# Chunks of two on-chip activation tensors laid 64 bytes further apart

## The chip, the cores and the metric

The program runs on one core of one Trainium2 chip. The metric is the device time of one launch in microseconds (us). Two runs of the kernel before took 2256.53 and 2257.57 us, median 2257.05 us. Numbers of the profile are of one execution of the same program.

The engines are TensorE (PE in the profile; its loads of the stationary operand are listed apart, as PEld), VectorE (DVE), ScalarE (ACT), GpSimd (POOL, idle here) and SyncE (SP, which only issues DMAs).

## The reference

What is computed is a stack of two blocks of two layers each on one sequence of T = 256 tokens with D = 1024 channels, in float32. Each layer is

```
h = rmsnorm(x, g1);   x = x + 0.5 * (silu(h @ w1) * (h @ w3)) @ w2       # FFN, 1024 -> 2816 -> 1024
h = rmsnorm(x, g_mix); p = h @ w_in                                       # 8 chunks of 128 channels
x = x + merge(mixers of p, gated by sigmoid(p)) @ w_o
h = rmsnorm(x, g2);   x = x + 0.5 * (silu(h @ w1b) * (h @ w3b)) @ w2b     # FFN again
```

In block 1 the mixers are a Fourier mix, a short convolution and a pooling mix; in block 2 they are a sliding-window attention and a gated linear attention. Block 1 ends with one more rmsnorm. Nearly all arithmetic is in the eight FFNs and in the projections of the mixers.

## The kernel before, in words

**Split products.** TensorE works on float32r operands. To keep float32 accuracy every operand is split into a high part and a low part, and each product is made of three matmuls: high by high, high by low, low by high. Weights arrive by DMA in `raw` (3 slots of 8192 bytes per partition); ScalarE copies a slot into the high half of `split_w` (line 1176), VectorE subtracts to make the low half (line 1646), in a ring of 4 slots.

**Activations, turned.** The normalised input of a stage lies in `xt`: for each of 8 chunks of 128 channels it holds 256 high values and behind them 256 low values per partition, that is 512 float32 or 2048 bytes per chunk. ScalarE writes the high part of a chunk (line 1188), VectorE the low part (line 1661), chunk by chunk, with 256 elements each. The product of the first FFN half, silu(gate) * up, lies in `ht_hi` and `ht_lo`: 22 chunks of 256 values or 1024 bytes each; ScalarE writes a chunk of the first (line 1253) and VectorE one of the second (line 1791).

**Two kinds of product.** They differ in which operand sits in the array (stationary) and which streams through it (moving).

- *FFN, first half* (`hidden_chunks`, lines 666 and 667; for the very first units `hidden_high` and `hidden_low`, lines 677 and 685): weights are stationary, `xt` moves. For each chunk c of `xt` and each of 2 column groups one matmul streams the whole chunk, 512 columns, against the high weights, and one streams its high half, 256 columns, against the low weights. So a chunk is used by 4 matmuls in a row, then comes the next chunk.
- *All else* (`blocks`, lines 602 to 604): 128 columns of the activation are stationary, the weights move, 512 columns at a time. For each chunk and each of 2 token halves there are three matmuls (602: high by high, 603: high by low weights, 604: low by high weights). So a chunk is used by 6 matmuls in a row. The activation is `xt` for the input projections of the mixers, `ht_hi`/`ht_lo` for the second half of an FFN, and small tensors (`bz`, `fq`, `pl`, `mt`, `oa`, `ob`) for the output projections of the mixers.

Every matmul has its own load of 128 stationary columns, 512 bytes per partition. In the trace the load for the next matmul starts together with the matmul at work.

**One odd form.** In block 2 two units of input weights (`kv` and `glr`) are 272 columns wide. Their four chunks lie packed in a slot of `split_w`, that is 272 * 4 = 1088 bytes apart. They are the only moving operands of the float32r kind in this kernel, besides one of 4 matmuls (line 1010), whose chunks don't lie at multiples of 512 bytes from the stationary ones.

**Places in memory.** Tensors are laid one behind the other in each partition, in the order in which `build` makes them, and those of stages that never live together share places (`ffn`, `mix1`, `mix2`). Worked out from the sizes in `build`, `split_w`, `xt`, `ht_hi`, `ht_lo` and all stationary tensors of the output projections start at an address that leaves 128 when divided by 512. Two `spacer` tensors ahead of them hold no data.

**What sets the order.** Each engine runs its own hand-written list; semaphores tie them. Nothing in the lists depends on addresses.

Of the kernel before, what the change touches and what calls it, by code (L numbers as in the profile page):

```python
# [21 lines left out]
F32R = mybir.dt.float32r  # L22
# [5 lines left out]
P = 128  # L28
T = 256
MT = T // P  # L30
D = 1024
DC = D // P
FF = 2816
FG = FF // 256
FC = FF // P
EPS = 1e-6
WARM = 11
PAIR = (0, 2, 1)
SPACER = 40
RAW = 3  # L40
HL = 4

# [133 lines left out]
def build(nc, a, known):  # L176

    ctx = ExitStack()
    counts = Counts()

    def semaphore(name):
        return ctx.enter_context(nc.semaphore(name))
# [7 lines left out]
    with ctx:  # L190
        def sb(stack, name, shape, dt=F32):
            return stack.enter_context(nc.sbuf_tensor(name, shape, dt))


        raw = sb(ctx, "raw", [P, RAW, 2048])
        split_w = sb(ctx, "split_w", [P, HL, 2, 2048], F32R)
        whi, wlo = split_w[:, :, 0, :], split_w[:, :, 1, :]
        x = sb(ctx, "x", [P, MT, D])
        xt = sb(ctx, "xt", [P, DC, 2, T], F32R)
        xt_hi, xt_lo = xt[:, :, 0, :], xt[:, :, 1, :]  # L200
        ident = sb(ctx, "ident", [P, P])

# [10 lines left out]

        sb(ctx, "spacer", [P, SPACER])
        tables2 = ExitStack()
# [16 lines left out]
        first.close()  # L232

        ffn = ExitStack()
        ht_hi = sb(ffn, "ht_hi", [P, FC, T], F32R)
        ht_lo = sb(ffn, "ht_lo", [P, FC, T], F32R)
        gate = sb(ffn, "gate", [P, 2, T])
        up = sb(ffn, "up", [P, 2, T])
        low = sb(ffn, "low", [P, 2, 2, T])
# [92 lines left out]

        raw_in = [semaphore(f"raw_in{r}") for r in range(RAW)]
        hi_done = semaphore("hi_done")
# [37 lines left out]
        def units(e, u, extra=0):  # L372

            return e.unit(u) + 1 + extra

        def loaded(e, u):

            return 32 * (e.unit(u) // RAW + 1) - 16

# [32 lines left out]
        def _(eng):  # L412
# [5 lines left out]
            def load(u, halves):  # L418

                r = e.unit(u) % RAW  # L420
                eng.wait_ge(w_ready, units(e, u))
# [157 lines left out]
        def _(eng):  # L579
# [7 lines left out]
            def blocks(u, block, p, split, chunks, start, stop, used, cols=512, beside=False, ready=True):  # L587
# [5 lines left out]
                if block == 0 and ready:  # L593
                    eng.wait_ge(w_ready, units(e, u, RAW))
                for i, c in enumerate(chunks):
# [13 lines left out]
            def last_blocks(u, p, split, chunks):  # L609

                hi, lo = split
                slot = u % HL
                eng.wait_ge(w_ready, units(e, u, RAW))
                for m in range(MT):
# [1804 lines left out]
```

## Time and profile before

| what | value |
|---|---|
| runs | 2256.53 and 2257.57 us |
| span of the profiled execution, first to last instruction | 2255.2 us |
| that span against the median of the runs, 2257.05 us | 1.85 us less |
| TensorE busy | 2249.8 us |
| VectorE, ScalarE busy | 1546.0 us, 1238.9 us |
| matmuls | 11686 |
| DMA | 417.61 MB, mean 185 GB/s |

A matmul's listed duration (about 390 ns for 512 columns) is longer than its turn on the engine, since matmuls overlap. What a stream of them costs is read from the starts: the time from one start to the next, best over a dozen of them, since the starts are given to 0.01 us. That time is called the *interval* here. The granted clock is 1.00 in all stretches shown, which is 2.4 GHz; at one column per cycle 512 columns would be 213.3 ns, 272 columns 113.3 ns and 256 columns 106.7 ns. What an interval has beyond that is called its *excess*.

### The profile page before, as it was taken

What the parts mean: (1) busy time and instruction counts of PE and PEld (TensorE: products, weight loads), DVE (VectorE), ACT (ScalarE), POOL (GpSimd) and SP (SyncE); (2) the same over time, 40 slices, a digit from 0 to 9 for tenths busy, and PEclk for the clock granted to TensorE, in tenths of its full rate; (3) what the DMA queues carried; (4) which work ended last, traced back from release to release, by engine and by line L of the source; (5) the groups of instructions that cost most, each with busy time, mean ns of one, the idle gap of its engine ahead of it and who ended that gap; (6) DMA issues with size and microseconds to landing.
All of it is one profiled execution on the core that took longest, in us unless ns stands there. A gap on an engine that the chain in (4) does not pass through costs nothing.

```text
span 2255.2 us, 28960 instructions
## 1 busy us (share of the span) xinstructions
PE 2249.8 (100%) x11686; PEld 1920.7 (85%) x11686; DVE 1546.0 (69%) x2179; ACT 1238.9 (55%) x1489; POOL 0.2 (0%) x4
## 2 busy tenths in 40 slices
PE   9999999999999999999999999999999999999999
PEld 8888888888888888888888888888888888888887
DVE  7764567765774566775776599767657747976773
ACT  7644445554653544654554576465555537755652
POOL 0000000000000000000000000000000000000000
PEclk9999999999999999999999999999999999999999
DMA  7556455555555455554555553545555555345553
GB/s 264 205 198 219 168 191 175 196 196 174 191 187 205 168 175 199 187 197 169 201 190 202 192 169 129 206 155 191 206 177 187 185 180 195 109 172 196 184 191 126
DMA packets 176213, 417.61 MB, mean 185 GB/s; under 512 B 16816, under 2 KB 20784, under 8 KB 176080
## 3 DMA queue, kind: packets, MB, share of 16 engines
q1 hardware_dynamic: 175936, 415.76, 53.3%
q8 instruction: 92, 1.51, 0.3%
q14 instruction: 41, 0.34, 0.0%
q10 hardware_dynamic: 144, 0.00, 0.0%
HBM read 414.66 MB, written 1.05 MB: 184 GB/s over the span
## 4 chain that ended last, share of the span: by engine, by line
PE 98%; DMA 1%; DVE 0%; SPq 0%; ACT 0%; issue 0%; DVEq 0%
PE psum L666 25%; PE psum L602 17%; PE psum L604 17%; PE psum L603 17%; PE psum L667 13%; PE psum L677 3%; PE psum L634 2%; PE psum L685 2%; PE psum L976 1%; DMA xt_in<-t_xt_dram 0%; PE psum L797 0%; DMA raw<-t_gate_up_1a_dram 0%; PE psum L954 0%; PE psum L817 0%; PE psum L944 0%; PE psum L966 0%
## 5 line engine op out<-in xcount | busy, mean ns | idle before, releaser
L1646 DVE TENSOR_TENSOR split_w<-raw,split_w 128x2048 fp32r<-128x2048 f32 (+1 forms) x405 | 881.1, 2182 | 285.8 <-ACT split_w L1176 284.9
L1176 ACT ACTIVATE split_w<-raw 128x2048 fp32r<-128x2048 f32 (+1 forms) x405 | 736.2, 1828 | 311.1 <-PE psum L604 288.2
L666 PE MATMUL psum<-xt,split_w 128*128 128x512 f32 x2464 | 859.2, 393 | 0.1
L667 PE MATMUL psum<-xt,split_w 128*128 128x256 f32 x2464 | 689.2, 280 | 0.0
L666 PEld LDWEIGHTS psum<-xt,split_w 128*128 128x128 f32 x2464 | 461.2, 187 | 104.3 <-DVE split_w L1646 1.3
L667 PEld LDWEIGHTS psum<-xt,split_w 128*128 128x128 f32 x2464 | 465.3, 189 | 0.3
L602 PE MATMUL psum<-split_w,xt 128*128 128x512 f32 (+1 forms) x736 | 289.5, 393 | 0.0
L604 PE MATMUL psum<-split_w,xt 128*128 128x512 f32 (+1 forms) x736 | 283.7, 385 | 0.0
L603 PE MATMUL psum<-split_w,xt 128*128 128x512 f32 (+1 forms) x736 | 283.6, 385 | 0.0
L602 PE MATMUL psum<-split_w,ht_hi 128*128 128x512 f32 x700 | 272.9, 390 | 0.0
L604 PE MATMUL psum<-split_w,ht_lo 128*128 128x512 f32 x700 | 272.5, 389 | 0.0
L603 PE MATMUL psum<-split_w,ht_hi 128*128 128x512 f32 x700 | 272.5, 389 | 0.0
L1775 DVE TENSOR_TENSOR gate<-psum,low 128x256 f32<-128x256 f32 x176 | 74.5, 423 | 155.3 <-ACT low L1242 155.1
L602 PEld LDWEIGHTS psum<-split_w,xt 128*128 128x128 f32 x736 | 138.4, 188 | 28.9 <-issue 3.0
L604 PEld LDWEIGHTS psum<-split_w,xt 128*128 128x128 f32 x736 | 138.2, 188 | 28.1
L1242 ACT ACTIVATE low<-psum 128x512 f32<-128x512 f32 x176 | 104.5, 594 | 103.7 <-PE psum L667 94.3
L603 PEld LDWEIGHTS psum<-split_w,xt 128*128 128x128 f32 x736 | 138.4, 188 | 25.6
L1248 ACT ACTIVATE gate<-gate 128x256 f32<-128x256 f32 x176 | 72.9, 418 | 158.4 <-DVE gate L1780 158.4
L604 PEld LDWEIGHTS psum<-split_w,ht_lo 128*128 128x128 f32 x700 | 131.4, 188 | 27.3
L602 PEld LDWEIGHTS psum<-split_w,ht_hi 128*128 128x128 f32 x700 | 131.4, 188 | 27.2
L603 PEld LDWEIGHTS psum<-split_w,ht_hi 128*128 128x128 f32 x700 | 131.4, 188 | 26.9
L1253 ACT ACTIVATE ht_hi<-hid 128x256 fp32r<-128x256 f32 x176 | 72.6, 417 | 91.4 <-DVE hid L1785 91.4
(278 smaller groups left out, 1951.2 us busy)
## 6 DMA issues: line engine op xcount, KB each, us to landing
raw<-w_in_dram SPq DMA_DIRECT2D x180, 512.0 KB, 4.4
raw<-t_gate_up_1b_dram SPq DMA_DIRECT2D x88, 512.0 KB, 4.1
raw<-t_gate_up_2a_dram SPq DMA_DIRECT2D x88, 512.0 KB, 4.1
raw<-t_gate_up_2b_dram SPq DMA_DIRECT2D x88, 512.0 KB, 4.1
raw<-t_gate_up_1a_dram SPq DMA_DIRECT2D x84, 512.0 KB, 4.1
raw<-ffn_w_down_dram SPq DMA_DIRECT2D x80, 512.0 KB, 4.2
raw<-w_a_dram SPq DMA_DIRECT2D x40, 512.0 KB, 4.4
raw<-w_b_dram SPq DMA_DIRECT2D x40, 512.0 KB, 4.4
```

The costliest lines, as they stand in the source:

```text
L602: nc.tensor.matmul(pair(p, m)[:, out], hi[:, c, t], whi[:, slot, w], start=first, stop=False)
L603: nc.tensor.matmul(pair(p, m)[:, out], hi[:, c, t], wlo[:, slot, w], start=False, stop=False)
L604: last = nc.tensor.matmul(pair(p, m)[:, out], lo[:, c, t], whi[:, slot, w], start=False, stop=final)
L666: nc.tensor.matmul(bank, whi[:, slot, w], xt[:, c, :, :], start=c == 0, stop=False)
L667: last = nc.tensor.matmul(bank[:, 0:T], wlo[:, slot, w], xt_hi[:, c, :], start=False, stop=c == DC - 1)
L677: nc.tensor.matmul(pair(p, j), whi[:, u % HL, first:first + P], xt[:, c, :, :], start=c == 0, stop=False)
L1176: nc.scalar.activation(whi[:, u % HL, 0:n], raw[:, r, 0:n], ACT.Copy).then_inc(hi_done, 1)
L1242: nc.scalar.activation(low[:, b % 2, :, :], psum[:, first:first + 2, T:2 * T], ACT.Copy).then_inc(low_done, 1)
L1248: nc.scalar.activation(gate[:, b % 2, :], gate[:, b % 2, :], ACT.Silu).then_inc(gate_done, 1)
L1253: nc.scalar.activation(ht_hi[:, b, :], hid[:, b % 2, :], ACT.Copy).then_inc(ht_hi_done, 1)
L1646: nc.vector.tensor_tensor(wlo[:, u % HL, 0:n], raw[:, r, 0:n], whi[:, u % HL, 0:n], ALU.subtract).then_inc(w_ready, 1)
L1775: return nc.vector.tensor_tensor(out[:, b % 2, :], bank[:, 0:T], low[:, b % 2, j, :], ALU.add)
```

## The change

Chunks of `xt` get 16 float32 of unused space behind their 512, chunks of `ht_hi` and `ht_lo` 16 behind their 256. The names are bound to views that leave the unused part out, so that all code that reads and writes them is as it was. Chunks of `xt` then lie 2112 bytes apart, those of `ht_hi` and `ht_lo` 1088. What is allocated behind `xt` moves up by 8 * 64 = 512 bytes, and `ht_lo` moves by 22 * 64 = 1408 bytes more.

```diff
@@ -37,6 +37,7 @@
 WARM = 11
 PAIR = (0, 2, 1)
 SPACER = 40
+PAD = 16
 RAW = 3
 HL = 4
@@ -196,7 +197,7 @@
         x = sb(ctx, "x", [P, MT, D])
-        xt = sb(ctx, "xt", [P, DC, 2, T], F32R)
+        xt = sb(ctx, "xt", [P, DC, 2 * T + PAD], F32R)[:, :, 0:2 * T].rearrange("p c (two t) -> p c two t", two=2)
         xt_hi, xt_lo = xt[:, :, 0, :], xt[:, :, 1, :]
@@ -232,8 +233,8 @@
         ffn = ExitStack()
-        ht_hi = sb(ffn, "ht_hi", [P, FC, T], F32R)
-        ht_lo = sb(ffn, "ht_lo", [P, FC, T], F32R)
+        ht_hi = sb(ffn, "ht_hi", [P, FC, T + PAD], F32R)[:, :, 0:T]
+        ht_lo = sb(ffn, "ht_lo", [P, FC, T + PAD], F32R)[:, :, 0:T]
         gate = sb(ffn, "gate", [P, 2, T])
```

The lists of instructions of all engines are the same before and after, form by form; only addresses and the line numbers of the source (one more) differ.

## Rows read from the trace of the kernel before

**Rows 1.** The page: busy time by engine, share of the span, instructions.
```profile
PE 2249.8 (100%) x11686; PEld 1920.7 (85%) x11686; DVE 1546.0 (69%) x2179; ACT 1238.9 (55%) x1489; POOL 0.2 (0%) x4
```
**Rows 2.** The page: the chain that ended last, shares of the span by engine.
```profile
PE 98%; DMA 1%; DVE 0%; SPq 0%; ACT 0%; issue 0%; DVEq 0%
```
**Rows 3.** Waits of TensorE: engine, line, waited for, us in total, times, longest.
```profile
PE psum L1153 <- DVE junk L2302: 1.3, 1, 1.3
PE psum L677 <- DVE xt L1677: 0.6, 1, 0.6
PE psum L677 <- ACT split_w L1176: 0.2, 1, 0.2
```
**Rows 4.** Groups of TensorE by line and form: count, busy us, mean ns.
```profile
L666 PE MATMUL psum<-xt,split_w 128*128 128x512 f32 x2464 | 859.2, 393 | 0.1
L667 PE MATMUL psum<-xt,split_w 128*128 128x256 f32 x2464 | 689.2, 280 | 0.0
L602 PE MATMUL psum<-split_w,xt 128*128 128x512 f32 x704 | 280.4, 398 | 0.0
L602 PE MATMUL psum<-split_w,ht_hi 128*128 128x512 f32 x700 | 272.9, 390 | 0.0
L677 PE MATMUL psum<-xt,split_w 128*128 128x512 f32 x352 | 85.9, 392 | 0.8 <-DVE xt L1677 0.6 <-ACT split_w L1176 0.2
```
**Rows 5.** Timeline, TensorE, second FFN half, even running: start us, duration us, line.
```profile
698.75 0.39 PE L602 MATMUL psum<-split_w,ht_hi 128*128 128x512 f32 x1
...
700.79 0.39 PE L602 MATMUL psum<-split_w,ht_hi 128*128 128x512 f32 x1
```
**Rows 6.** Timeline, TensorE, first FFN half, even running: 8 pairs of lines 666 and 667.
```profile
384.22 0.39 PE L666 MATMUL psum<-xt,split_w 128*128 128x512 f32 x1
...
386.99 0.39 PE L666 MATMUL psum<-xt,split_w 128*128 128x512 f32 x1
```
**Rows 7.** Timeline, TensorE, first FFN half, ahead of the norm's spreading matmul.
```profile
366.96 0.40 PE L666 MATMUL psum<-xt,split_w 128*128 128x512 f32 x1
...
371.91 0.40 PE L666 MATMUL psum<-xt,split_w 128*128 128x512 f32 x1
```
**Rows 8.** Timeline, TensorE, the first matmuls of a second FFN half.
```profile
486.49 0.39 PE L602 MATMUL psum<-split_w,ht_hi 128*128 128x512 f32 x1
...
488.57 0.39 PE L602 MATMUL psum<-split_w,ht_hi 128*128 128x512 f32 x1
```
**Rows 9.** Timeline, TensorE, the moving chunks that lie 1088 bytes apart.
```profile
1284.23 0.28 PE L602 MATMUL psum<-split_w,xt 128*128 128x272 f32 x1
1284.35 0.30 PE L603 MATMUL psum<-split_w,xt 128*128 128x272 f32 x1
1284.49 0.29 PE L604 MATMUL psum<-split_w,xt 128*128 128x272 f32 x1
...
1287.23 0.28 PE L602 MATMUL psum<-split_w,xt 128*128 128x272 f32 x1
```
**Rows 10.** Line 603: times, duration ns min/median/max, first and last start.
```profile
L603 PE MATMUL psum<-split_w,ht_hi x700: 387/389/398, 130.6 to 2248.7; 128*128 128x512 f32 x175
```
**Rows 11.** Busy us by stretch: PE, PEld, DVE, ACT, POOL; granted clock, DMA share, GB/s.
```profile
380.00:460.00 80.00, 80.00 (x463) 70.55 (x462) 59.99 (x89) 48.64 (x62) 0.00 (x0) 1.00 0.54 188
700.00:715.00 15.00, 15.00 (x72) 12.52 (x71) 10.85 (x10) 6.47 (x8) 0.00 (x0) 1.00 0.48 167
```
**Rows 12.** Costliest groups, the two splits of a weight slot: count, busy us, mean ns.
```profile
L1646 DVE TENSOR_TENSOR split_w<-raw,split_w 128x2048 fp32r<-128x2048 f32 (+1 forms) x405 | 881.1, 2182 | 285.8 <-ACT split_w L1176 284.9
L1176 ACT ACTIVATE split_w<-raw 128x2048 fp32r<-128x2048 f32 (+1 forms) x405 | 736.2, 1828 | 311.1 <-PE psum L604 288.2
```

## The prediction

> **What bounds the kernel now.** I read the page's busy times first: TensorE is busy 2249.8 us of a span of 2255.2 us, VectorE 69% and ScalarE 55% of it [rows 1]. The chain of waits says the same from the other side: 98% of what ended last is TensorE, 1% is the DMA at the start [rows 2]. TensorE's list of waits is empty but for 1.3 + 0.6 + 0.2 us at the start [rows 3]. So TensorE hands one matmul to the next from first to last, and the time is the sum of the intervals between their starts. A change of addresses can move the end only through those intervals; VectorE, ScalarE and DMA have a third of the span in hand and more.
>
> What an interval is made of is read from the timeline. In the even part of a second FFN half the starts 698.75 and 700.79 us lie 9 matmuls apart [rows 5]: 2.04 / 9 = 226.7 ns for 512 columns, an excess of 13.3 ns over the 213.3 ns that the columns need at a granted clock of 1.00 [rows 11]. In the even part of a first half 8 pairs of 512 + 256 columns take 386.99 - 384.22 = 2.77 us [rows 6]: 346 ns a pair, 320 for the columns, again 13 ns of excess per matmul. Two more facts bear on the change. The intervals are this even while VectorE and ScalarE are busy in 75% and 61% of the stretch (59.99 and 48.64 of 80.00 us) and the DMA engines in 54% [rows 11], so other engines' accesses don't show in them. And the same forms at the same spacing of chunks also run slower: 14 pairs ahead of the norm's spreading matmul take 371.91 - 366.96 = 4.95 us, 353.6 ns each, 7.2 more than in the even part [rows 7], and the first 9 matmuls of a second half take 488.57 - 486.49 = 2.08 us, 231.1 ns each, 4.4 more [rows 8]. So the excess isn't a constant of the form: it depends on how a matmul and the load beside it fall against each other. What I cannot read is whether their addresses are part of that.
>
> **The change part by part.**
>
> *Instructions.* None is added, removed or moved. No operand changes its shape: the writers of `xt`, `ht_hi` and `ht_lo` and the matmuls touch one chunk at a time, and the gap lies between chunks. Cost 0 on every queue, no DMA changes its size or target's shape. 3328 more bytes per partition are taken and nothing else has to give way.
>
> *Tensors that only move.* All behind `xt` shift by 512 bytes and `ht_lo` by 1408 more. The durations of VectorE and ScalarE would have to grow by a third of the span to reach the end, so 0.
>
> *Where chunks lie against each other.* This is the one term. Chunk c now starts 64 * c bytes further on, and a load (512 bytes per partition) and the stream beside it meet at another distance, unless 64 * c is a multiple of 512: for one chunk in 8 nothing changes, counted modulo 512. Matmuls concerned, from the counts by form: those with `xt` moving, 2 * (2464 + 352) = 5632; with `xt` stationary, 3 * 704 + 96 of 272 columns = 2208; with `ht` stationary, 3 * 700 + 12 = 2112 [rows 4]; lines 603 and 604 count as line 602 does and line 685 as line 677, and the 96 and the 12 are the 272-column form and the last weights' lines 618 to 620. Together 9952, and 7/8 of them is 8700. The output projections of the mixers keep their distances and serve as a control.
>
> The price per matmul isn't in the trace, so I bound it. *Nearest row:* the 272-column matmuls, whose moving chunks lie 1088 bytes apart, so that their distance to the stationary operand shifts by 0, 64, 128 and 192 bytes modulo 512 as the change would have it. 24 of them take 1287.23 - 1284.23 = 3.00 us [rows 9], 125.0 ns each; columns (113.3) plus the usual excess (13.3) would be 126.7. So the row says 1.7 ns less, and 8700 * 1.7 = 15 us less. *Upper near end:* the uneven running of rows 7 and 8 becomes the rule, 7.2 ns a pair and 4.4 ns a matmul. *Far ends:* the whole excess goes, -13.3 ns, or each matmul costs what the slowest ones do, 398 against a median of 389 ns, +9 ns [rows 10]. I take 0: the nearest row lies 1.7 ns from it, and inside that row I see no step where the distance changes, only single intervals that jump about (the second is 0.14 us, its neighbours 0.12) and a mean that stays.
>
> A rule of the Trainium skill bears on this. The row shows 226.7 ns from start to start for 512 columns [rows 5]. The page TensorE: Matmul & The Clock Gate (part 2, step 1, and "Wait — 56ns, not 53.3ns?") says that TensorE has two independent read ports, that loading the next tile's weights takes no bandwidth from the running matmul, and that back-to-back matmuls of 512 columns start 215.7 ns apart. By that rule no address could matter and the sum is 0 as well. But this trace shows 11 ns more per matmul than the page's gap, and a second speed of the same form, so here the ports are not shown to be free of each other, and I give the rivals below more room than the page would.
>
> **Sum.** Against the span: 2255.2 + 0 + 0 + 0 = 2255.2 us; the median of the runs is 1.85 us above it, so 2257 us.
>
> **The rivals.**
>
> *Slower: the even running is lost at each chunk.* In `blocks` a chunk lasts for 6 matmuls, while the settling seen in rows 8 takes about 9; in the first FFN halves a chunk lasts for 4. If a new distance throws the matmuls out of step each time, they never settle. Price: 2816 pairs * 7/8 * 7.2 ns = 18 us and (2112 + 2208) * 7/8 * 4.4 ns = 17 us, together 35 us: 2292 us. For it: two speeds exist for one form. Against it: rows 9, where new distances every 6 matmuls go with a mean no worse than usual.
>
> *Slower by over 2%: the distances themselves are bad.* If a load and a stream that are out of line disturb each other more than now, by the 9 ns of rows 10, the sum is 8700 * 9 = 78 us: 2335 us. It passes the 2% from 45.1 us on, that is from 5.2 ns per matmul. For it: the second interval of rows 9. Against it: the mean of the same rows.
>
> *A little faster, as the 272-column row:* 2257 - 15 = 2242 us. For it: that row is the only one of this kind with shifted chunks. Against it: its form differs in columns too, and 1.7 ns may be the form's.
>
> *Much faster: the excess is a clash of equal distances and the shift ends it.* Up to 8700 * 13.3 = 116 us: 2141 us. For it: but for rows 9 and four matmuls of line 1010 the operands of all float32r matmuls lie in line modulo 512, and in even running all of these show the same 13.3 ns. Against it: rows 9 are out of line and still have 11.7 ns.
>
> *The change doesn't do what it says:* if distances modulo something larger than the shift decided, or if the address played no part at all, it would be my forecast again, with the same time.
>
> **How the numbers follow.** 2% of 2257 us is 45 us, about what a measurement of this kernel tells from no change at least; here the two runs lie 1.04 us apart, so smaller differences will be readable too. Chances: no effect of the distance (2254 to 2260 us) 0.36; even running lost, wholly or in part (2262 to 2300) 0.26; a little faster (2235 to 2252) 0.18; bad distances (over 2302) 0.12; clash ended, wholly or in part (below 2212) 0.08. The first is the likeliest and gives the time, 2257 us. The range 2238 to 2296 us takes in the first three. The chances: faster by over 2% 0.08, within 2% 0.80, slower by over 2% 0.12.
>
> **What would show each step.** In the profile after: counts by form as before; TensorE still at 98% of the chain and without waits. Forecast: intervals of `ht` and `xt` matmuls of 226.7 ns and pairs of 346 ns in the same stretches. Settling rival: pairs near 353 ns throughout and `ht` intervals near 231 ns with the first of each chunk out of step, while the `mt`, `bz` and `ob` matmuls keep 226.7. Bad distances: the same control even, intervals above 232 ns, the excess going up and down with c and even again at chunks 0, 8 and 16 of `ht`. Small gain: 225 ns. Clash ended: intervals towards 213 ns. My forecast is wrong if the mean interval of the changed forms moves by more than 1 ns. It is wrong in another way if they keep their intervals and TensorE begins to wait for `split_w`, which would mean that the copies on VectorE (2182 ns each in the mean now) or ScalarE (1828 ns) slowed [rows 12].

## The result, and the profile after

| | before | after |
|---|---|---|
| median of the runs | 2257.05 us | 2283.30 us (2282.89 and 2283.71) |
| span of the profiled execution | 2255.2 us | 2281.1 us |
| TensorE busy | 2249.8 us | 2275.6 us |

The changed kernel is slower: ratio 1.0116, 95% interval 1.0097 to 1.0135, which is 26.25 us. That is inside the range of 2238 to 2296 us and inside the 2% that I called "within", but the effect is clear of the noise, and I had forecast none.

The page of after, busy time and the chain (what stood in [rows 1, 2]):

```profile
PE 2275.6 (100%) x11686; PEld 1924.9 (84%) x11686; DVE 1546.8 (68%) x2179; ACT 1239.4 (54%) x1489; POOL 0.2 (0%) x4
...
PE 99%; DMA 1%; DVE 0%; SPq 0%; ACT 0%; issue 0%; DVEq 0%
```

The same number of matmuls takes 25.8 us more, and VectorE and ScalarE work within 1 us as long as before. The waits of TensorE (engine, line, waited for, total us, times, longest), which answer to [rows 3]:

```profile
PE psum L1154 <- DVE junk L2303: 1.3, 1, 1.3
PE psum L678 <- DVE xt L1678: 0.6, 1, 0.6
PE psum L678 <- ACT split_w L1177: 0.4, 1, 0.4
```

Nothing new is waited for. Every line number is one higher than before. By form (count, busy us, mean ns of one), against [rows 4]:

```profile
L667 PE MATMUL psum<-xt,split_w 128*128 128x512 f32 x2464 | 866.3, 394 | 0.1
L668 PE MATMUL psum<-xt,split_w 128*128 128x256 f32 x2464 | 693.1, 281 | 0.0
L603 PE MATMUL psum<-split_w,xt 128*128 128x512 f32 x704 | 282.9, 402 | 0.0
...
L603 PE MATMUL psum<-split_w,ht_hi 128*128 128x512 f32 x700 | 276.1, 394 | 0.0
...
L603 PE MATMUL psum<-split_w,mt_hi 128*128 128x512 f32 x128 | 50.6, 395 | 0.0
```

The mean of the `ht` form goes from 390 to 394 ns and that of `xt` stationary from 398 to 402. The `mt` form, the control whose distances are as they were, stays at 50.5 and 50.6 us for its 128. What counts is read from the starts. Two stretches serve for all kernels here: 160 pairs (one matmul of 512 columns and one of 256) of the first half of the second FFN, and 96 matmuls (16 chunks) of its second half. Before (start us, duration us, line), first the pairs, then `ht`:

```profile
381.10 0.39 PE L666 MATMUL psum<-xt,split_w 128*128 128x512 f32 x1
...
436.57 0.39 PE L666 MATMUL psum<-xt,split_w 128*128 128x512 f32 x1
```
```profile
489.25 0.39 PE L602 MATMUL psum<-split_w,ht_hi 128*128 128x512 f32 x1
...
511.01 0.39 PE L602 MATMUL psum<-split_w,ht_hi 128*128 128x512 f32 x1
```

That is 55.47 / 160 = 346.7 ns a pair and 21.76 / 96 = 226.7 ns. After:

```profile
385.22 0.39 PE L667 MATMUL psum<-xt,split_w 128*128 128x512 f32 x1
...
441.22 0.39 PE L667 MATMUL psum<-xt,split_w 128*128 128x512 f32 x1
```
```profile
494.40 0.39 PE L603 MATMUL psum<-split_w,ht_hi 128*128 128x512 f32 x1
...
516.62 0.39 PE L603 MATMUL psum<-split_w,ht_hi 128*128 128x512 f32 x1
```

A pair takes 56.00 / 160 = 350.0 ns where it took 346.7, and an `ht` matmul 22.22 / 96 = 231.5 ns where it took 226.7. Summed over all starts of the trace by form, the matmuls with `xt` moving take 7.7 us more, those with `xt` stationary 8.1 us, those with `ht` stationary 10.1 us: 25.9 us, the whole difference of the spans.

### The profile page after: what moved, and what is told of

The parts are those of the page before. It is cut to its first block, busy times and chain, and to the rows that moved or that the text cites. A ratio compares the mean times of both kernels' runs of the same rounds, so it can differ in the third digit from the quotient of the medians.

```text
span 2281.1 us, 28960 instructions
## 1 busy us (share of the span) xinstructions
PE 2275.6 (100%) x11686; PEld 1924.9 (84%) x11686; DVE 1546.8 (68%) x2179; ACT 1239.4 (54%) x1489; POOL 0.2 (0%) x4
## 4 chain that ended last, share of the span: by engine, by line
PE 99%; DMA 1%; DVE 0%; SPq 0%; ACT 0%; issue 0%; DVEq 0%
PE psum L667 25%; PE psum L603 17%; PE psum L605 17%; PE psum L604 17%; PE psum L668 13%; PE psum L678 3%; PE psum L635 2%; PE psum L686 2%; PE psum L977 1%; DMA xt_in<-t_xt_dram 0%; PE psum L798 0%; DMA raw<-t_gate_up_1a_dram 0%; PE psum L955 0%; PE psum L818 0%; PE psum L945 0%; PE psum L967 0%
## 5 line engine op out<-in xcount | busy, mean ns | idle before, releaser
L603 PE MATMUL psum<-split_w,ht_hi 128*128 128x512 f32 x700 | 276.1, 394 | 0.0
L604 PE MATMUL psum<-split_w,ht_hi 128*128 128x512 f32 x700 | 275.9, 394 | 0.0
```

The costliest lines, as they stand in the source:

```text
L603: nc.tensor.matmul(pair(p, m)[:, out], hi[:, c, t], whi[:, slot, w], start=first, stop=False)
L604: nc.tensor.matmul(pair(p, m)[:, out], hi[:, c, t], wlo[:, slot, w], start=False, stop=False)
```

## The experiments

Three theories stood after the result. **Out of step:** what costs is a distance that is new at each chunk. **Distance:** each distance between the two operands, taken modulo some number, has its own cost, whether it changes or not. **Own place:** where one operand lies by itself counts. "Distance" is always the start of the activation minus the start of the weights.

### One padded tensor at a time (a1, a2)

Each is the kernel before with `PAD = 16` and one half of the change:

```diff
-        xt = sb(ctx, "xt", [P, DC, 2, T], F32R)
+        xt = sb(ctx, "xt", [P, DC, 2 * T + PAD], F32R)[:, :, 0:2 * T].rearrange("p c (two t) -> p c two t", two=2)
```

Expected of the above alone: 

> Only the chunks of xt lie 64 bytes further apart, those of ht_hi and ht_lo as before. If the loss is the sum of what each padded tensor's own matmuls lose (out of step or bad distances alike), the xt share of the trace after is all that is lost: 5632 matmuls with xt moving (+7.7 us) and 2112 with xt stationary (+8.1 us), so about 2273 us (2270 to 2276); intervals of the ht matmuls back at 226.9 ns. If instead the shift of the tensors behind xt cost something, the ht matmuls would stay slow and the time would be above 2277 us.

Measured: 2273.03 us, ratio 1.0068 (1.0053 to 1.0083), +15.3 us against the 2257.75 us of the kernel before, measured together with it.

The other half of the change alone:

```diff
-        ht_hi = sb(ffn, "ht_hi", [P, FC, T], F32R)
-        ht_lo = sb(ffn, "ht_lo", [P, FC, T], F32R)
+        ht_hi = sb(ffn, "ht_hi", [P, FC, T + PAD], F32R)[:, :, 0:T]
+        ht_lo = sb(ffn, "ht_lo", [P, FC, T + PAD], F32R)[:, :, 0:T]
```

Expected: 

> Only the chunks of ht_hi and ht_lo lie 64 bytes further apart. Sum of shares: the 2112 ht matmuls go from 226.9 to about 232 ns, +10.1 us, so about 2267 us (2265 to 2270); pairs of the first FFN half at 346.7 ns. With a1 the two gains must add up to the 26.25 us of the whole change within 2 us, if no third part plays.

Measured: 2267.19 us, ratio 1.0042 (1.0027 to 1.0057), +9.4 us. The two add up to 24.7 us of 26.25. So the loss is where the padded tensors are used; moving what lies behind `xt` by 512 bytes shows no cost (the `ht` matmuls of a1 keep 226.7 ns).

### A distance that doesn't change (a3, a4)

```diff
+        sb(ctx, "shift", [P, 16])
         x = sb(ctx, "x", [P, MT, D])
```

Expected: 

> No chunk is padded; 64 bytes are put behind split_w, so that xt, ht and all else stand at a constant distance of 64 bytes modulo 512 from the weights. Out-of-step theory (a NEW distance at each chunk keeps the matmuls from settling): the distance never changes, so after a few matmuls all run even, 226.7 ns and 346.7 ns a pair, 2257 us (2254 to 2262). Distance theory (each unequal distance has its own cost): ht, xt, mt, ob matmuls all lose 2 to 5 ns also in even running, as in the chunks c = 1 of the run after (352.5 ns a pair), so 2275 to 2300 us. Rival that gains: an unequal but constant distance ends the clash, below 2240 us.

Measured: 2295.73 us, ratio 1.0169 (1.0154 to 1.0184), 38 us slower with no chunk padded at all. The same 96 `ht` matmuls:

```profile
496.31 0.39 PE L603 MATMUL psum<-split_w,ht_hi 128*128 128x512 f32 x1
...
518.71 0.39 PE L603 MATMUL psum<-split_w,ht_hi 128*128 128x512 f32 x1
```

22.40 / 96 = 233.3 ns, and this is even running, not settling: it holds through all passes over `ht`, and the forms `mt`, `ob` and `xt` stationary slow as well. The out-of-step theory can't be the whole cause: here no distance is ever new. Whether a new distance costs something on top is taken up below (b4).

```diff
+        sb(ctx, "shift", [P, 16])
         raw = sb(ctx, "raw", [P, RAW, 2048])
```

Expected: 

> 64 bytes are put ahead of raw, so that weights and activations move together: all distances are as in the kernel before, only each tensor's own place modulo 512 is 192 in place of 128. Both theories on distances expect 2257 us (2256 to 2259) and the intervals of before. If the place of one operand by itself decided, it would differ, by the size of a3.

Measured: 2257.29 us, ratio 0.9999 (0.9990 to 1.0009). Weights and activations moved together cost nothing: it is the distance between them, not the place of either.

### Other constant distances (b1 to b3, c2, c3, d2, d3)

Each is the edit of a3 with another size of `shift`. Expected of 256, 128 and 448 bytes:

> Constant distance of 256 bytes, no chunk padded. In the profile of the change the pairs of the first FFN half repeat after 4 chunks, that is after 256 bytes, while the ht intervals repeat only after 8 chunks. If 256 bytes is the period for both kinds, 2257 us (2255 to 2260). If it is the period for a moving activation alone: pairs at 346.7 ns, the 512-column matmuls of blocks at 230 to 233 ns, 2270 to 2287 us. If any unequal distance costs what 64 bytes costs: 2296 us.

> Constant distance of 128 bytes. Each unequal distance costs alike: 2296 us, blocks at 233.3 ns. Cost falls with the distance: between 2257 and 2290 us. A better distance than zero exists: below 2250 us. From the profile of the change, chunk 2 of xt has pairs of 349.6 ns against 352.5 in chunk 1, so I expect the middle case, about 2285 us.

> Constant distance of 448, which is 64 bytes to the other side modulo 512. If the sign of the distance doesn't count, 2296 us as with 64 bytes. If it counts (the load runs ahead of the stream or behind it), the two kinds of matmul change places: pairs of the first half lose 6 ns or more and the blocks 2 to 3 ns: 2275 to 2300 us, with the pair at 353 ns and the blocks at 229 to 230 ns. Gain: below 2250 us.

Of 32 and 224 bytes:

> Constant distance of 32 bytes. If whole blocks of 64 bytes count, 32 behaves as 0 or as 64: 2257 or 2296 us. If the cost goes with the distance, between them, about 2276 us. A distance better than 0 below 64 bytes would show as less than 2250 us, with 512-column intervals below 226.7 ns; I give that 15%.

> Constant distance of 224, 32 bytes to the other side modulo 256. If it behaves as 192 (448 modulo 256): 2281 us with pairs of 353 ns. If as 0: 2257 us. Between: 2268 us. Gain: below 2250 us, 15%.

Of 96 and 160 bytes:

> Constant distance of 96 bytes, to complete the map at steps of 32. From its neighbours 64 (2296) and 128 (2294 us): 2290 to 2300 us. If a better distance than 0 is anywhere, it is here or at 160: below 2255 us, 7%.

> Constant distance of 160 bytes. From its neighbours 128 (2294) and 192 (2281 us): 2280 to 2298 us. Below 2255 us, 7%.

Measured, with the intervals from the same two stretches of each trace (granted clock 1.00 in all; columns alone would be 213.3 and 320 ns):

| distance | time, us | ratio (95%) | `ht` matmul, ns | pair, ns |
|---|---|---|---|---|
| 0 (before) | 2257 | 1 | 226.7 | 346.7 |
| 32 | 2285.29 | 1.0122 (1.0106 to 1.0139) | 233.3 | 346.7 |
| 64 | 2295.73 | 1.0169 (1.0154 to 1.0184) | 233.3 | 348.9 |
| 96 | 2298.90 | 1.0185 (1.0156 to 1.0215) | 234.4 | 350.0 |
| 128 | 2293.62 | 1.0158 (1.0141 to 1.0175) | 232.5 | 351.1 |
| 160 | 2287.17 | 1.0134 (1.0104 to 1.0163) | 233.3 | 346.7 |
| 448 (192 modulo 256) | 2281.42 | 1.0105 (1.0088 to 1.0122) | 229.0 | 353.3 |
| 224 | 2301.65 | 1.0194 (1.0179 to 1.0209) | 233.3 | 353.3 |
| 256 | 2257.34 | 1.0001 (0.9992 to 1.0010) | 226.7 | 346.7 |

At 256 bytes all is as at 0 (first the pairs, then `ht`):

```profile
381.45 0.39 PE L667 MATMUL psum<-xt,split_w 128*128 128x512 f32 x1
...
436.92 0.39 PE L667 MATMUL psum<-xt,split_w 128*128 128x512 f32 x1
```
```profile
489.59 0.39 PE L603 MATMUL psum<-split_w,ht_hi 128*128 128x512 f32 x1
...
511.35 0.39 PE L603 MATMUL psum<-split_w,ht_hi 128*128 128x512 f32 x1
```

So the distance counts modulo 256 bytes, for both kinds of matmul. (One of the four runs at 128 took 4587.58 us, twice the time of the other three; it is left out, and nothing here explains it.) No distance that I tried is better than 0, and all between cost 24 to 44 us. The two kinds don't follow one rule: summed over the whole trace, the matmuls with `xt` moving take 982.7 us at 0, no more at 32 and 160 (981.6 and 982.0), and 990.3 to 998.4 at the other five. My expectations missed for 32 (2257 or 2296 were named, or 2276; it is 2285), for 128 (about 2285 was likeliest; it is 2294) and for 224 (no case reached 2302), so the cost doesn't simply grow with the distance; at 448 the sign did count, as the expectation had it, with the pairs at 353 ns. The pairs have more than one lasting speed at one distance: at 64 bytes they ran at 348.9 ns in this FFN and, with the same addresses, at (681.26 - 624.73) / 160 = 353.3 ns in the next:

```profile
624.73 0.40 PE L667 MATMUL psum<-xt,split_w 128*128 128x512 f32 x1
...
681.26 0.39 PE L667 MATMUL psum<-xt,split_w 128*128 128x512 f32 x1
```

So the column of pairs is exact for its stretch alone.

The rows behind the 448 line show the trade: the blocks lose least here and the pairs as much as anywhere (first the pairs, then `ht`):

```profile
382.05 0.40 PE L667 MATMUL psum<-xt,split_w 128*128 128x512 f32 x1
...
438.58 0.40 PE L667 MATMUL psum<-xt,split_w 128*128 128x512 f32 x1
```
```profile
492.21 0.39 PE L603 MATMUL psum<-split_w,ht_hi 128*128 128x512 f32 x1
...
514.19 0.39 PE L603 MATMUL psum<-split_w,ht_hi 128*128 128x512 f32 x1
```

56.53 / 160 = 353.3 ns and 21.98 / 96 = 229.0 ns.

### A gap that keeps the distance (c1)

The edit of a2, with 256 bytes in place of 64:

```diff
-PAD = 16
+PAD = 64
```

Expected: 

> Chunks of ht_hi and ht_lo get 256 bytes of gap in place of 64 (1280 bytes from chunk to chunk), xt as before. Distance theory with a period of 256 bytes: every chunk is in line again, so 2257 us (2256 to 2259) although the chunks are no longer next to each other. If a gap between chunks by itself, or a distance that is new at each chunk, cost something: 2267 us as in the run with only ht padded by 64.

Measured: 2257.65 us, ratio 1.0000 (0.9991 to 1.0010). The 96 matmuls of `ht`:

```profile
490.35 0.39 PE L603 MATMUL psum<-split_w,ht_hi 128*128 128x512 f32 x1
...
512.11 0.39 PE L603 MATMUL psum<-split_w,ht_hi 128*128 128x512 f32 x1
```

21.76 / 96 = 226.7 ns. Padding itself is harmless when it is a multiple of 256 bytes.

### Which of the two operands' matmuls shows it (b4, c4, d1)

```diff
+        sb(ffn, "shift", [P, 16])
         ht_lo = sb(ffn, "ht_lo", [P, FC, T], F32R)
+        sb(ffn, "shift_back", [P, 112])
```

Expected: 

> Only ht_lo stands 64 bytes off; ht_hi and all else is in line. While line 603 streams, the low stationary for line 604 is loaded; while lines 604 and 602 stream, a high one is loaded. If the load beside the stream is what clashes, the ht intervals of line 603 rise (by 6 to 15 ns) and those of 602 and 604 by little; the 700 of them cost 4 to 10 us: 2261 to 2267 us. If the address of the operand a matmul itself works with counted, line 604 would rise instead and 603 would stay at 227 ns.

Measured: 2265.34 us, ratio 1.0034 (1.0023 to 1.0046). The size is as expected, the place isn't. The three lines, here numbered 604 to 606 for 602 to 604:

```profile
L606 PE MATMUL psum<-split_w,ht_lo 128*128 128x512 f32 x700 | 278.1, 397 | 0.0
...
L605 PE MATMUL psum<-split_w,ht_hi 128*128 128x512 f32 x700 | 274.4, 392 | 0.0
L604 PE MATMUL psum<-split_w,ht_hi 128*128 128x512 f32 x700 | 273.2, 390 | 0.0
```

It is the matmul that works with the displaced stationary that slows most (389 to 397 ns), not the one beside which that stationary is loaded (389 to 392). In the trace's own nanoseconds the intervals of the three repeat as 236 (ht_lo), 228 and 229. Summed over starts, the `ht` matmuls take 8.9 us more than before, 12.7 ns for each of the 700 displaced ones, where a constant distance of 64 bytes costs 6.6 ns (a3): a distance that differs from the neighbours' costs something on top. Since each third matmul disturbs the next two, I made the disturbance rare: chunk 10 of `ht_lo` alone lies 64 bytes off, in a tensor of its own.

```diff
-        ht_lo = sb(ffn, "ht_lo", [P, FC, T], F32R)
+        ht_lo_main = sb(ffn, "ht_lo", [P, FC, T], F32R)
+        sb(ffn, "shift", [P, 16])
+        ht_lo_apart = sb(ffn, "ht_lo_apart", [P, T], F32R)
+        sb(ffn, "shift_back", [P, 112])
+        ht_lo = OneApart(ht_lo_main, ht_lo_apart, 10)
```

(`OneApart`, not shown, hands out `ht_lo_apart` for chunk 10 and `ht_lo_main` for all others.)

Expected: 

> Only chunk 10 of the low ht tensor lies 64 bytes off; its stationary is loaded twice in each of the 16 passes over ht. The time can't tell it (2257 to 2260 us); the intervals can. If the load beside the stream clashes, the first interval off 226 to 227 ns in each pass is that of line 603 at chunk 10, beside which the low stationary is loaded. If the address of the operand that a matmul itself works with counts, or if a start in the trace stands one matmul ahead of its stream, the first one off is that of line 604. After chunk 10 the intervals should settle back to 226.7 ns within about 10 matmuls.

Measured: one time, 2257.93 us. The starts around chunk 10 in the second FFN (lines 616 to 618 stand for 602 to 604; the displaced tensor has its own name):

```profile
500.36 0.39 PE L618 MATMUL psum<-split_w,ht_lo 128*128 128x512 f32 x1
500.59 0.39 PE L616 MATMUL psum<-split_w,ht_hi 128*128 128x512 f32 x1
500.82 0.39 PE L617 MATMUL psum<-split_w,ht_hi 128*128 128x512 f32 x1
501.04 0.40 PE L618 MATMUL psum<-split_w,ht_lo_apart 128*128 128x512 f32 x1
501.28 0.39 PE L616 MATMUL psum<-split_w,ht_hi 128*128 128x512 f32 x1
501.51 0.39 PE L617 MATMUL psum<-split_w,ht_hi 128*128 128x512 f32 x1
501.74 0.40 PE L618 MATMUL psum<-split_w,ht_lo_apart 128*128 128x512 f32 x1
```

0.23, 0.23, 0.22 and then 0.24 us: the first long interval begins at the displaced matmul itself, in all 16 passes, with 235 or 236 ns in the trace's own nanoseconds after 225 or 226 for the one ahead of it. After seven intervals (236, 229, 229, 236, 228, 232, 231, then 227) it runs even again, some 34 ns lost for two displaced matmuls. The displaced chunk's load lies wholly beside line 617, whose interval is 225 or 226 ns:

```profile
500.82 0.19 PEld L618 LDWEIGHTS psum<-split_w,ht_lo_apart 128*128 128x128 f32 x1
```

Two readings were left: **theory A** of the next expectation, a load that clashes with the stream beside it, if starts stood one matmul ahead; and **theory B**, something between the two operands of one matmul. The last run displaces a moving operand in place of a stationary one: the low weights of one unit.

```diff
...
-                        nc.tensor.matmul(pair(p, m)[:, out], hi[:, c, t], wlo[:, slot, w], start=False, stop=False)
+                        wl = wlo_apart[:, w] if is_apart(e, u) else wlo[:, slot, w]
+                        nc.tensor.matmul(pair(p, m)[:, out], hi[:, c, t], wl, start=False, stop=False)
...
```

(Not shown: `wlo_apart` lies 64 bytes off behind the FFN tensors, VectorE writes that unit's low half there, and `is_apart` picks one unit in each second FFN half.)

Expected: 

> In one unit of each second FFN half (the third of 11) the LOW weights, which move only in line 603, stand 64 bytes off; all stationary operands are in line. In the run with one ht_lo chunk off, the first late interval was that of line 604, whose own stationary was the one off. Theory A, the load clashes with the stream beside it and a start in the trace stands one matmul ahead of its stream: with the moving operand of 603 off, the clash lies beside the stream of 603 and shows one interval later, at line 604. Theory B, the interval that shows it is that of the matmul with the displaced operand: the first late one is that of line 603, and 604 follows only by what settling does. Time 2257 to 2260 us either way.

Measured: one time, 2257.62 us. The start of the displaced unit in the second FFN (lines 609, 611, 612 stand for 602, 603, 604):

```profile
497.53 0.39 PE L609 MATMUL psum<-split_w,ht_hi 128*128 128x512 f32 x1
497.76 0.40 PE L611 MATMUL psum<-wlo_apart,ht_hi 128*128 128x512 f32 x1
497.99 0.40 PE L612 MATMUL psum<-split_w,ht_lo 128*128 128x512 f32 x1
498.23 0.39 PE L609 MATMUL psum<-split_w,ht_hi 128*128 128x512 f32 x1
```

Rounded starts show it faintly; in the trace's own nanoseconds the interval at the unit's first displaced matmul is 236 or 237 ns, after 226 or 227 for the one ahead of it, in all 8 passes, and the one behind it is 240 or 241. So the displaced matmul's own interval shows it first here too, and theory A, which wanted line 604's first, falls. The load beside the same matmul's stream, taken without a shift, would fit here but not in c4. What c4 and d1 have in common is that the first late interval is that of the matmul whose own two operands stand at another distance.

That this distance alone sets an interval isn't shown. The longest interval of d1, 240 or 241 ns, is that of line 612, whose own operands are in line. And displaced weights count the other way: this distance is -64, that is 192 modulo 256, at which `ht` runs at 229.0 ns when it is constant, not at 236. So the first intervals behind a change of distance are not the price of the distance in even running. Which accesses of memory meet, the runs don't show.

## Why the prediction was wrong, point by point

- **What bounds the kernel** was right. TensorE remains the chain, without new waits, and all of the change is in intervals.
- **Instructions, and tensors that only move: 0.** Right: instruction counts are the same, and the 24.7 us of a1 and a2 leave 1.5 of 26.25 us, which is within the interval of the measurement (1.0097 to 1.0135 is 22 to 30 us).
- **The count**, 8700 matmuls whose distance changes, was a little high, since I took it modulo 512. The period is 256, so it is about 3/4 of 9952, 7500. I also took both halves of `ht` to go by the chunk number alone. But 22 padded chunks put `ht_lo` 1408 bytes further on, 128 modulo 256, so in the kernel after line 604 stands at another distance than lines 602 and 603 of the same chunk: for `ht` the distance changes at every third matmul and not only every sixth.
- **The price, "I take 0", is the step that failed.** It is 25.9 us / 7500 = 3.5 ns per matmul. I took 0 because of the nearest row, the 272-column matmuls at 125.0 ns [rows 9], whose distances are 0, 192, 128 and 64 modulo 256 from chunk to chunk. The mean of this form hardly reacts to the distance. The kernel after shows it: there `xt` is padded by the same 64 bytes as the weights' chunks, so that all these matmuls are in line, and the same 24 start at

```profile
1299.91 0.29 PE L603 MATMUL psum<-split_w,xt 128*128 128x272 f32 x1
...
1302.90 0.28 PE L603 MATMUL psum<-split_w,xt 128*128 128x272 f32 x1
```

  that is (1302.90 - 1299.91) / 24 = 124.6 ns, 0.4 less than out of line (over all 96 matmuls of this form it is 124.7 against 125.0). For `ht` at 512 columns the same four distances cost 3.7 ns in the mean (0, 6.6, 5.8 and 2.3). Over all traces that mean of 96 stays between 124.7 and 125.6 ns. So it says nothing of 512 and 256 columns, and the 1.7 ns that I read as a gain belong to the form: it has them in line too. A row that has the suspected property is evidence only if the form is known to react to it, and no row of the trace before could show that.
- **The single intervals that I set aside** as jumping about did hold a sign. In the trace's own nanoseconds the six matmuls of the first chunk of rows 9 take 120, 135, 125, 121, 124, 127 and those of the third 125, 127, 127, 123, 128, 125, the same in each pass to within 1 ns. In the kernel after, every chunk from the third on repeats 121, 134, 125, 122, 124, 122; with a constant 64 bytes (a3) the 135 stands in the second chunk, which is in line there. So the pattern follows the distance while its mean stays, and the 0.14 us that the bad-distances rival called evidence is an interval of a chunk in line.
- **The settling rival** (2292 us) gave the nearest numbers: it wanted `ht` at 231.1 ns and pairs near 353, and 231.5 and 350.0 came. That is mostly luck: its mechanism isn't the main one. A distance that never changes costs more (a3, 38 us), and one that changes by 256 bytes at each chunk costs nothing (c1). The padding deals out distances 0, 64, 128 and 192 in about equal parts: the mean of the four constant kernels is (2257 + 2296 + 2294 + 2281) / 4 = 2282 us against 2283.3 measured. These four include some 2 us in the output projections, which the padding spares. By sums over starts the mean of the four lies 8.3 us above before for `xt` moving, 6.7 for `xt` stationary and 7.4 for `ht`, where the change cost 7.7, 8.1 and 10.1. So about 4 of the 26 us lie in `blocks` beyond what the distances cost when constant, most of it in `ht`, where the distance changes every third matmul; b4 shows that changes have such a price. This share is worked out, not measured alone.
- **The bad-distances rival** was right that the distances themselves cost, with too high a price: 9 ns at each, where the constant distances give 2 to 8 ns for `ht`, and 0 to 7 ns for a pair. Its picture of a load that disturbs the stream beside it is not borne out (c4).
- **The little gain and the ended clash** fell: none of the eight other distances goes below 226.7 ns for `ht` or 346.7 for a pair. The excess of 13.3 ns that remains in line stays unexplained.
- **The rule of the Trainium skill.** By its page TensorE: Matmul & The Clock Gate (part 2, step 1, and "Wait — 56ns, not 53.3ns?") a load takes no read bandwidth from the running matmul and back-to-back matmuls of 512 columns start 215.7 ns apart. It was a reason to hold 0 for likely. The traces have 226.7 to 234.4 ns for one form, depending on a distance alone, so the measurement decides: for float32r operands in this kernel the gap isn't a constant of the number of columns.

## What to carry to other kernels

When TensorE is the bound, compare the interval from start to start with the columns' own time, and if there is an excess, try the stationary and the moving operands at equal addresses modulo 256 bytes; here every other distance in steps of 32 cost 1.1 to 1.9%, and padding chunks by 64 bytes cost 1.2%. This is shown for float32r matmuls of 512 and 256 columns with a load for each; other types were not tried, and the mean of the 272-column form hardly moved. A pad or a small tensor put ahead of the operands can do this by accident, and no wait or engine in the profile will name it: only the intervals do. Before a nearest row is used as a price, ask whether its form is known to react at all, and look at its single intervals and not only at their mean.

## What the runs showed of the hardware that I had not expected

- The interval of a float32r matmul of 512 columns depends on the distance of its operands modulo 256 bytes: 226.7 ns at 0 and at 256, and 229.0 to 234.4 ns at seven others (activation stationary). Moving both together changes nothing (2257.29 us).
- The two orders of operands react differently: at 32 and 160 bytes the pairs with the activation moving lose nothing (346.7 ns) and those with it stationary 6.6 ns; at 448 bytes it is 6.6 ns a pair and 2.3 ns.
- The mean of the 272-column form hardly reacts (124.7 to 125.6 ns in all traces), though its single intervals follow the distance.
- Two displaced matmuls, three apart, disturb seven intervals before the even running returns (c4), and a displaced matmul among others in line costs about twice what it costs when all are displaced alike (12.7 against 6.6 ns, b4 and a3).
- At one distance there can be two lasting speeds: 348.9 and 353.3 ns a pair at 64 bytes, and at 0 346.7 ns against 353.6 over 14 pairs [rows 7].
